# A decoder layer step on one core: 64-row shift and mask products, a separate mask load, and the last eight down panels by token halves

## The reference

```python
  z = x @ w_in   (one combined projection; columns split among four head groups)
  A  Conformer convolution module, 256 channels: GLU -> causal depthwise conv (width 31) -> LayerNorm over channels -> swish -> pointwise
...
  mixer output = concat(A, B, C, D) @ w_out ;  x <- LN(alpha*x + mixer)
  x <- LN(alpha*x + relu(x @ w_up)^2 @ w_down)
...
def masked_softmax(s, mask):
    s = jnp.where(mask, s.astype(jnp.float32), -jnp.inf)
    m = jnp.max(s, axis=-1, keepdims=True)
    m = jnp.where(jnp.isfinite(m), m, 0.0)
    e = jnp.exp(s - m)
    d = jnp.sum(e, axis=-1, keepdims=True)
    return e / jnp.where(d > 0, d, 1.0)
```

## Time and profile before

| | us |
|---|---|
| median of three runs | 788.78 (784.44 to 791.16) |
| the profiled execution | 785.52 |
| its span, first to last instruction | 783.8 |
| PE busy | 746.2 (95%) |
| DVE busy | 426.7 (54%) |
| ACT busy | 281.7 (36%) |
| POOL busy | 198.4 (25%) |

### The profile page before, as it was taken

The page is one execution under the profiler, slowest core; times in us unless marked ns, Lnnn a source line. Parts: engine busy times, 40 slices in busy tenths (PEclk is TensorE's granted clock), DMA queues, the critical chain, the costliest instruction groups (busy, mean ns, idle before and its releaser), DMA issues.

```text
span 783.8 us, 17110 instructions
## 1 busy us (share of the span) xinstructions
PE 746.2 (95%) x6808; PEld 657.7 (84%) x6808; DVE 426.7 (54%) x715; ACT 281.7 (36%) x542; POOL 198.4 (25%) x252
## 2 busy tenths in 40 slices
PE   9999999987987999999999999999999999999992
PEld 8999989764554545579989999999999999999991
DVE  4878984555545532446865666433562345523535
ACT  5232234544535322533345444222341233312124
POOL 0000635002324553003737722001110011100083
PEclk9999999999999999999999999999999999999996
DMA  9657772558779885421342233422333222333102
GB/s 333 186 154 180 207 208 74 201 182 292 278 262 326 252 269 170 145 82 55 86 184 82 81 101 94 129 81 83 85 104 106 84 81 81 109 96 93 54 2 109
DMA packets 64473, 113.27 MB, mean 145 GB/s; under 512 B 18921, under 2 KB 36074, under 8 KB 63722
## 3 DMA queue, kind: packets, MB, share of 16 engines
q1 hardware_dynamic: 58378, 95.92, 39.8%
q0 software_dynamic: 6016, 16.26, 5.9%
HBM read 107.72 MB, written 6.52 MB: 146 GB/s over the span
## 4 chain that ended last, share of the span: by engine, by line
PE 81%; DVE 8%; ACT 4%; issue 3%; DMA 2%; POOLq 0%; SPq 0%; ACTq 0%; POOL 0%; DVEq 0%
PE psum L724 58%; PE psum L733 3%; PE psum L810 2%; PE psum L842 2%; PE psum L1006 2%; PE psum L779 2%; PE psum L813 2%; PE psum L994 1%; DVE wL L1512 1%; DVE yc L1582 1%; DMA moba_hi<-in_moba_pages 1%; DMA moba_lo<-in_moba_pages 1%; DMA wgate<-in_w_gate 1%; ACT xres L1370 1%; PE psum L1042 1%
## 5 line engine op out<-in xcount | busy, mean ns | idle before, releaser
L1512 DVE TENSOR_TENSOR wL<-raw,wH 128x1024 fp32r<-128x1024 f32 (+1 forms) x92 | 117.3, 1275 | 95.3 <-ACT wH L1157 95.3
L1157 ACT ACTIVATE wH<-raw 128x1024 fp32r<-128x1024 f32 (+1 forms) x92 | 94.1, 1023 | 120.5 <-PE psum L724 119.9
L724 PE MATMUL psum<-oxH,wH 128*128 128x260 f32 (+1 forms) x512 | 105.0, 286 | 1.4 <-DVE wL L1512 0.9
L724 PE MATMUL psum<-oxH,wL 128*128 128x260 f32 (+1 forms) x512 | 103.9, 284 | 0.0
L724 PE MATMUL psum<-oxL,wH 128*128 128x260 f32 (+1 forms) x512 | 103.4, 283 | 0.0
L724 PE MATMUL psum<-hidH,wL 128*128 128x260 f32 x512 | 103.2, 283 | 0.0
L724 PE MATMUL psum<-hidH,wH 128*128 128x260 f32 x512 | 103.2, 283 | 0.0
L724 PE MATMUL psum<-hidL,wH 128*128 128x260 f32 x512 | 103.0, 283 | 0.0
L1476 POOL TENSOR_TENSOR hsq<-relu 128x520 f32<-128x520 f32 x32 | 33.8, 1056 | 218.7 <-ACT relu L1338 218.7
L724 PE MATMUL psum<-opH,wH 128*128 128x260 f32 x400 | 85.6, 295 | 3.5 <-DVE wL L1512 1.4
L724 PEld LDWEIGHTS psum<-oxH,wH 128*128 128x128 f32 x512 | 79.5, 189 | 3.3 <-issue 2.4
(11 more groups left out here) (357 smaller groups left out, 1128.6 us busy)
## 6 DMA issues: line engine op xcount, KB each, us to landing
raw<-in_panels SPq DMA_DIRECT2D x88, 512.0 KB, 3.6
nsa_ring<-in_nsa_pages SPq DMA_DIRECT2D x128, 96.0 KB, 2.2
moba_hi<-in_moba_pages SPq DMA_DIRECT2D x36, 256.0 KB, 4.6
moba_lo<-in_moba_pages SPq DMA_DIRECT2D x36, 256.0 KB, 4.7
moba_lo<-in_moba_pages POOLq DMA_DIRECT2D x28, 256.0 KB, 5.1
moba_hi<-in_moba_pages POOLq DMA_DIRECT2D x28, 256.0 KB, 5.1
selV<-in_selv_pages SPq DMA_DIRECT2D x80, 32.0 KB, 3.0
xres<-in_xT SPq DMA_DIRECT2D x8, 260.0 KB, 5.5
```

Of the source, the lines that this page charges most:

```text
L724: last = mm(out[:, hf, 0:cols], w, x[:, k, hf * HALF:hf * HALF + cols], start=(t == 0 and j == 0), stop=(t == KT - 1 and j == 2))
L1157: fn(wtiles(wH, wH3, n).rearrange("p a b -> p (a b)")[:, cols], raw[:, n % NRAW, cols], ACT.Copy).then_inc(h_done, 1)
L1512: tt(wtiles(wL, wL3, n).rearrange("p a b -> p (a b)")[:, cols], raw[:, n % NRAW, cols], wtiles(wH, wH3, n).rearrange("p a b -> p (a b)")[: ...
```

## The change

**Shift and mask products over 64 rows.** The shift of a query now stands in rows 0 to 31 and again in 64 to 95, the rest of the rounding in 32 to 63 and 96 to 127, so that head e = 0 multiplies rows 0 to 63 and e = 1 rows 64 to 127. The shifts are put eight times side by side into a tile `XR`, and one transposition of 128 rows (step `lset`) replaces those of 12 and 4. The clearing of `shift` is gone. A mask product of 128 columns becomes two of 64, over 64 rows, for each head: four instructions. In the compressed column parts one product of 512 columns for each head replaces four of 128.

**Masks in a load of their own.** They leave `cst` and go as `mask_words` (128 x 544 words, 272 KB) into a part of `vec` that the convolution's and pool's weights held. `load_post` waits for the users of these weights and loads the masks ahead of winK; row part 0 waits for them.

**Token halves at the end.** The last eight down panels are run as 16 half panels (`mmh`, `evach`): first all eight for tokens 0 to 259, then for 260 to 519, each into one of four PSUM banks. Their eight split panels stay in SBUF, in four slots over the old oxH and oxL, three usual ones and one over hidH. `AHEAD` lists how many splits stand in each of the eight panels ahead (1, 1, 1, 1, 1, 3, 2, 2), and two more follow. The LayerNorm runs for each half; that of the first stands in the second half's panels, with its y writes. GpSimd still adds sums for both and subtracts for the first half, and does nothing behind the last sum of the second, where DVE subtracts all eight tiles.

```diff
+LAST = N_PANELS - KT
+AHEAD = [(LAST - 6,), (LAST - 5,), (LAST - 4,), (LAST - 3,), (LAST - 2,), (LAST - 1, LAST, LAST + 1), (LAST + 2, LAST + 3), (LAST + 4, LAST + 5)]
...
-    tl += [("ln", 1), ("lnv", 1), ("y", 0)]
+    tl += [("split", LAST + 6), ("split", LAST + 7)]
+    behind = {KT: [("ln", 1)], KT + 1: [("lnv", 1), ("ysub", 0)]}
+    behind |= {KT + 2 + q: [("y", 0, 2 * q), ("y", 0, 2 * q + 1)] for q in range(KT // 2)}
+    for q in range(2 * KT):
+        h, k = q // KT, q % KT
+        tl += [("mmh", q)] + ([("smean", 1 + h)] if k == 2 else []) + [("evach", q)] + tail(1 + h, k) + behind.get(q, [])
+    tl += [("ln", 2), ("lnv", 2)] + [("y", 1, k) for k in range(KT)]
...
+                    sp_.wait_ge(conv_done, 1)
+                    sp_.wait_ge(vtap, len(TAPS))
+                    sp_.wait_ge(cpw_mm, 2)
+                    sp_.wait_ge(pool_mm, 2)
+                    sp_.dma_start(mask_words[:, :], a["masks"]).then_inc(masks_in, 16)
                     sp_.dma_start(winK[:, :, :], a["winK"]).then_inc(win_in, 16)
...
+            def half_panel(q):
+
+                h, k = q // KT, q % KT
+                if q >= 4:
+                    read(pe, ("mmh", q - 4))
+                else:
+                    read(pe, ACC[max(m for m in range(len(ACC)) if PAIR[m] == q // 2)])
+                if h == 0:
+                    pe.wait_ge(l_done, split_no(LAST + k))
+                pe.wait_ge(hid_l_done, NG * KT)
+                w_h, w_l = wtiles(0, LAST + k), wtiles(1, LAST + k)
+                x_h, x_l = hidH[(NG - 1) % 2], hidL[(NG - 1) % 2]
+                for t in range(KT):
+                    for j, (w, x) in enumerate(((w_h, x_h), (w_h, x_l), (w_l, x_h))):
+                        last = mm(psum[:, q % 4, 0:HALF], w[:, t, :], x[:, t, h * HALF:(h + 1) * HALF],
+                                  start=(t == 0 and j == 0), stop=(t == KT - 1 and j == 2))
+                last.then_inc(mm_done, 1)
...
-                    for e in range(2):
-                        last = mm(psum[:, b + e, m - P:m], masks[:, M_ID:M_ID + P], masks[:, M_CAUS:M_CAUS + P],
-                                  start=False, stop=True, skip_group_check=True)
+                    for k in range(2):
+                        for e in range(2):
+                            half = slice(HD * e, HD * e + HD)
+                            last = mm(psum[:, b + e, m - P + HD * k:m - P + HD * k + HD], masks[half, M_ROW + k * P:M_ROW + (k + 1) * P],
+                                      masks[half, M_ID:M_ID + HD], start=False, stop=True, skip_group_check=True)
...
-                    r = (0 if kind == "moba" else H * BRANCH[kind]) + 2 * t + e
-                    mm(out[e], pick[:, r:r + 1].to_broadcast([P, keys]), shift[:, int(kind == "moba"), lo:T],
-                       start=False, stop=False, skip_group_check=True)
...
+                    r = H * BRANCH[kind] + 2 * t + e
+                    half = slice(HD * e, HD * e + HD)
+                    mm(out[e], pick[half, r:r + 1].to_broadcast([HD, keys]), shift[half, lo:T], start=False, stop=False, skip_group_check=True)
+                if kind == "cmp":
+                    for e in range(2):
+                        half = slice(HD * e, HD * e + HD)
+                        last = mm(out[e], masks[half, M_ID:M_ID + NCMP_P], masks[half, M_CMP:M_CMP + T], start=False, stop=True, skip_group_check=True)
+                else:
+                    for k in range(2):
+                        for e in range(2):
+                            half = slice(HD * e, HD * e + HD)
+                            last = mm(out[e][:, k * HD:(k + 1) * HD], masks[half, M_COL + k * P:M_COL + (k + 1) * P],
+                                      masks[half, M_ID:M_ID + HD], start=False, stop=True, skip_group_check=True)
...
-                    tt(shift[32:32 + hi - lo, n, :], psum[0:hi - lo, 2 + n, :], shift[0:hi - lo, n, :].bitcast(F32), ALU.subtract).then_inc(bfree[2 + n], 1)
+                    dve.wait_ge(xth_done, 1)
+                    for lo in (32, 96):
+                        low = slice(lo, lo + 32)
+                        last = tt(shift[low, :], psum[low, 2, :], shift[low, :].bitcast(F32), ALU.subtract)
+                    last.then_inc(bfree[2], 1)
...
+                    if n and k < 4:
+                        tt(xres[:, k + 4, cols], xres[:, k + 4, cols], dmean[:, cols], ALU.subtract).then_inc(vln, 1)
```

More of the change, by code:

```diff
@@ L116, in panel @@
         ahead = 2 if i >= OUT0 else 1
+        if i >= LAST - KT:
+            for m in AHEAD[i - LAST + KT]:
+                out += [("split", m)] + ([("load_panel", m + 2)] if m + 2 < N_PANELS else [])
+            return out + [("mm", i)] + list(mid) + [("evac", i)]
         if i + ahead < N_PANELS and i + ahead != OUT0:
@@ L252, in timeline @@
         tl += panel(i, [("smean", 0)] if i == OUT0 + 2 else []) + tail(0, i - OUT0)
-    for i in range(FF0, N_PANELS):
-        k = i - (N_PANELS - KT)
-        step = panel(i, [("smean", 1)] if k == 2 else [])
+    for i in range(FF0, LAST):
+        step = panel(i)
         if i == FF0:
@@ L258, in timeline @@
             step[at_:at_] = [("ln", 0), ("lnv", 0)]
-        tl += step + (tail(1, k) if k >= 0 else [])
+        tl += step
         if i - FF0 < KT:
@@ L269 @@
 Y_POOL_SUB = (3, 4, 5, 6, 7)
-Y_ORDER = range(KT)
+Y_SUB, Y_MUL = [], []
+for _q in range(KT):
+    Y_SUB.append(KT + 3 + (_q + 1 if _q < 4 else 2 * _q - 2))
+    Y_MUL.append(KT + 3 + (2 * _q + 5 if _q < 4 else _q + 9))
 ACC = []
@@ L672, in acc_wait @@
                 if n >= NACC1 and n < NACC1 + 2:
-                    for k in range(4):
+                    for k in range(3):
                         pe.wait_ge(bfree[k], len(USES[k]))
@@ L1049, in _ @@
                     if b == 0:
-                        pe.wait_ge(bfree[3], len(USES[3]))
+                        read(pe, ACC[max(m for m in range(NACC1) if PAIR[m] == 1)])
                         mm(psum[:, 3, :], zeros[:, :], Psel[:, 0, :], start=True, stop=False, skip_group_check=True)
@@ L1103, in _ @@
                     pe.wait_ge(xsum_done, n + 1)
-                    for hf in range(2):
+                    for hf in range(2) if n == 0 else (n - 1,):
                         last = mm(psum[:, 4 + hf, 0:HALF], mean1024[:, :], xsum[:, hf * HALF:(hf + 1) * HALF], start=True, stop=True)
@@ L2024, in layouts @@
     cst[:, C_ID:C_ID + P] = np.eye(P)
-    last = 16 * np.arange(NCMP_P) + 31
-    masks = [np.eye(P), np.where(p_[None, :] <= p_[:, None], 0.0, NEG)]
-    masks += [np.where(last[None, :] <= (i * P + p_)[:, None], 0.0, NEG) for i in range(QT)]
+    h_, q_ = np.arange(HD)[:, None], p_[None, :]
+    masks = [np.eye(HD)]
+    masks += [np.where(HD * k + h_ <= q_, 0.0, NEG) for k in range(2)]
+    masks += [np.where(q_ <= HD * k + h_, 0.0, NEG) for k in range(2)]
+    masks += [np.where((h_ >= NCMP_P) | (16 * h_ + 31 <= np.arange(T)[None, :]), 0.0, NEG)]
     high = (np.concatenate(masks, 1).astype(np.float32).view(np.uint32) >> 16).astype(np.uint16)
-    cst[:, C_MASK:C_COVER] = np.ascontiguousarray(high).view(np.float32)
+    mask_words = f(np.tile(high, (2, 1))).view(np.float32)
     for j in range(4):
```

240 lines of the change are left out of this document (143 added, 97 removed).

## The result

| | kernel before | changed kernel |
|---|---|---|
| median of five runs, us | 788.78 (784.44 to 791.16) | 778.70 (776.76 to 781.90) |
| ratio to before, 95% interval | | 0.9895 (0.9872 to 0.9919) |
| profiled execution, us (span) | 785.52 (783.8) | 781.36 (779.7) |

The gain is clear of zero; whether it is over or under 1% isn't settled by either interval. The forecast was 779.8 us, the range 774 to 787. The number is right. The account behind it is only partly right: TensorE lost nearly twice the work that I had summed for the attention, and more than half of that was given back, in waits and in a lower clock that I had priced at nothing.

A forecast was written before the change was run, and what follows sets the result against it. TensorE was taken to bound the attention's column part, and LayerNorm's serial chain the last 19 us. Attention -5.3 and end -3.7 make -9.0 us, from 788.8 to 779.8 us, range 774 to 787.

The forecast's parts named there:

- Shift products: Column part: 64-row pairs run together, saving 3.8 us of columns, second compressed part included, and 2.5 us of fixed cost.
- the constant: Shift products: 0.20 us left in each without its columns, partly a row-mode change; 2.5 us saved, bounds 0 to 5.
- Mask products: Column part, 24 places: four 64-column products replacing two of 128 cost 1.0 us more, bounds 0 to 3.1.
- Second compressed part: Column part: shift product falls by 0.23 us, eight L818 products (0.55 us) become a pair at 0.35; together 0.4 us saved.
- Start of the column part: Waiting for two DVE subtractions adds 0.67 us, shorter products give it back; net 0, bounds -0.3 and +0.7.
- PE has no wait for a page there: Column part: argument against rival A that TensorE does not wait for page loads; no cost booked.
- rival A: Column part: pairs don't run together, or page loads bind; only the end gains, 785 us. Chance 0.13.
- the attention's 5.3 us: Attention total: 3.8 and 2.5 us saved on shift products, 1.0 us lost on masks, start 0.
- Masks in their own load: Before row part 0: the separate mask load causes no wait; cost 0, or 0.8 us of PE if it lands late.
- End: Behind the last product: 12.9 us instead of 18.8, less 1.8 on PE, GpSimd 0.4 late; 3.7 us saved.
- rival B: End: GpSimd's second-half sums are 3 to 4 us late, so only the attention gains, 783.5 us. Chance 0.09.
- Rival C: Row and column parts: 64-column mask products without overlap and with a drain make it slower, some 797 us. Chance 0.06.

The follow-up runs named there:

- e6_mask128: e7 with causal mask products over 128 rows and 128 columns again, two instead of four; ratio to the kernel before 0.9890.
- e1: Kernel before plus only the attention part of the change, last panels and end as before; ratio to the kernel before 0.9946.
- e3: Changed kernel with two early out panels issued behind the last V page and eight page loads moved to GpSimd; ratio to the kernel before 0.9941.
- e7: Changed kernel with the second and third early out panels issued behind the last V page; ratio to the kernel before 0.9850, 774.3 us.
- e10: e7 with the last four page loads of the sixth batch on SP's queue instead of GpSimd's; ratio to the kernel before 0.9858.
- e12: e7 with the first token half's five subtractions on VectorE instead of GpSimd; ratio to the kernel before 0.9846.
- e5: e7 with shift products over 128 rows again, mask products left at 64 rows; ratio to the kernel before 0.9967.
- e8: The whole changed kernel, unaltered, measured a second time; ratio to the kernel before 0.9893.
- e9: e7 with both shift and causal mask products over 128 rows again; ratio to the kernel before 0.9940.
- e2: Kernel before plus only the token halves at the end, attention as before; ratio to the kernel before 0.9939.
- e4: Kernel before with the same two edits of panel order and page loads as e3; ratio to the kernel before 0.9987.
- e11: Kernel before with the one panel-order edit of e7; ratio to the kernel before 0.9973.

## Why the prediction was right, and where it was not

- **Shift products: under-sized.** I had 3.8 us for the columns and 2.5 of 0 to 5 for the constant. The columns were right: 0.66 to 0.23 us is one product's 0.23 us and the whole 0.20. The step that failed is "the row doesn't split it, so I take half". The whole constant went away, at every size. Over the four sizes the pair fell by 0.43, 0.36, 0.31 and 0.31 us, six of each: 8.5 us. One step of the reasoning was weaker than it read. Four L810 instructions at L813's 0.23 us would take 0.92 us one behind the other, so their 1.06 us speak for pairs that run together only with a factor of passes that no row gives. The 0.23 us of the changed pair is the first row here that shows it.
- **Mask products: wrong sign.** I charged 1.0 us. They gave 24 x 0.06 = 1.4 us in the column part, and e6_mask128 measured 3.1 in the whole kernel. With the neighbour's rows the same (64 ahead of small, 128 ahead of large) the four small ones cost half of the two large. Large masks behind 64-row shift products would even have cost 0.22 us (e6), so that there the small form saves 0.15 a place. My bounds reached from 0 to 0.13 dearer and had no place for a saving.
- **Second compressed part: right.** L889 0.34 us and L893 0.32, where I had 0.35 for both. Sum of TensorE's savings in the column part by the chain: 8.5 + 1.4 + 0.5 = 10.4 us; the busy time says 9.6.
- **Start of the column part: a small miss.** I had 0 (-0.3 to +0.7). TensorE's first score there waits 1.6 us for VectorE's two subtractions (0.8 before). In the profiled execution those four instructions then took 1.92 us instead of 1.06: the granted clock was 0.50 from 250.7 to 252.7 us (full speed is 2.4 GHz, the lower level 1.2, so these ran at the lower). TensorE had been busy 15.66 of the 23 us ahead, at a mean clock of 0.85. This isn't one execution's accident. Over the first 3 us of the column part the clock was 0.51 to 0.56 in seven of the ten traces with the two subtractions (after, e1, e3, e6, e7, e10, e12), and 1.00 in the other three (e5, e8, e9) and in all four with one (before, e2, e4, e11). From the busy time of e7_order against e8_after it costs about 1.4 us (82.80 against 81.42), which I had not priced. Why three were spared is open.
- **The path after the saving: the real miss.** "PE has no wait for a page there" was true of the trace of before (its weight load waited 0.3 us) and was used for after. With TensorE 10 us shorter, V pages at 0.73 us of SP's issue each became what the second half waits for, and the moba pages (0.90 us of issue each on GpSimd) cost another 1.1 to 1.8 us (after, e1, e7, e8). That is the second half of rival A, to which I gave 0.13; it took a part of the gain, not all of it. e1_att arrived with 4.2 us of the 10.4.
- **So the attention's 5.3 us came out near the 4.2 measured by two errors that cancel**: 5 us too little saved, and 6 us given back that I had not seen. In the trace of e1_att 3.9 us of these are idle time of TensorE (4.8 against 1.0) and about 1.4 the lower clock. That the number was right is, for this half of the forecast, luck.
- **Masks in their own load: right.** The first compressed row products start at 150.84 us, right behind a panel's, with no wait.
- **End: right in its terms but for one not charged.** 12.8 us from the last product (12.9 forecast), the reciprocal over 5.3 us behind the last product (5.1), 5.3 to the last scaling (5.3), the four half-width mean products 4 x 0.44 = 1.8 us in the stream (1.8), GpSimd 0.28 us late (0.4): the mean product starts 0.40 us behind the start of the last product, where products are 0.12 apart. GpSimd's margin was as thin as rival B feared: its last sum ends at 767.6. It was slowed as forecast, 0.94 us instead of 0.75 beside VectorE's multiplications, and VectorE as well, which I hadn't charged: three subtractions took 2.69 us beside GpSimd's five, against 0.34 us from start to start at the end of the kernel. The timed gain was 4.8 us (3.1 to 6.5) for 3.7.
- **Rival C (slower)** is refuted: e1_att is faster than the kernel before (0.9946), and no column part with small products is dearer than its large form in the chains.

## What to carry to other kernels

Price a TensorE instruction together with its neighbours: a small product in the row mode of the one ahead of it can be cheaper than half as many large ones in another mode, and two edits of that kind don't add up. Before a saving on the bound engine is booked, look at every queue that feeds the stretch and ask when it would be done if the engine asked earlier; a queue that ends 0.3 us behind the need is the next limit, however busy the engine looks. A new wait can cost twice, once as idle time and once as products at the lower clock behind it. And when large loads move forward because their queue is free, see which small loads they now overtake (argued from e3, not proved).

## What was not expected of the hardware

- A change of row mode costs 0.09 us in either direction at the bf16 masks, 0.20 to 0.26 us at the fp32 shift product behind a 64-row score (e5, e6, e9), and nothing visible at the page product behind a 64-row mask (1.00 us with and without).
- Four bf16 mask products over 64 rows and 64 columns, in two row halves, add 0.07 us to the chain, though each shows 0.19 us by itself (195 ns mean in the profile): they overlap. The two large ones show 0.22 us each and add 0.13.
- VectorE's and GpSimd's elementwise operations slow each other: 0.34 to about 0.9 us and 0.75 to 0.94 us for 260 columns.
- The start of the column part lay between 244.9 and 253.8 us in traces of kernels with the same attention code (after, e8, e3, e7, e10, e12). What differs ahead of it are waits for page loads and the clock that follows them. I take it for a large part of the scatter between runs; what sets it in one run or another wasn't tested.
